# Half of the output projection in seven block products instead of eight (Strassen-Winograd) for six of sixteen tile pairs

## The reference

```python
for l in range(DEPTH):
    h = rms_norm(x, norm_g[l])
    proj = jnp.einsum('bsd,dn->bsn', h, w_in[l])
    ...
    y = jnp.concatenate([y_a, y_b, y_c], axis=-1)
    x = x + jnp.einsum('bsm,md->bsd', y, w_out[l])
return x
```

## Time and profile before

| what | value |
|---|---|
| median of three executions | 1538.51 us |
| the profiled execution, its own time | 1538.53 us |
| its span | 1536.8 us |
| PE busy | 1532.3 us (100%) |
| DVE busy | 994.8 us (65%) |
| ACT busy | 753.3 us (49%) |
| POOL busy | 356.7 us (23%) |
| HBM read and written | 219 GB/s over the span |

### The profile page before, as it was taken

How to read it: one execution, slowest core, us unless ns; L and a number is a source line. 1 busy time by engine, 2 the same in 40 slices (tenths; PEclk the granted TensorE clock), 3 DMA queues, 4 the chain that set the end, 5 groups by cost and what they waited for, 6 DMA issues and landing times.

```text
span 1536.8 us, 18847 instructions
## 1 busy us (share of the span) xinstructions
PE 1532.3 (100%) x6996; PEld 1271.5 (83%) x6996; DVE 994.8 (65%) x1537; ACT 753.3 (49%) x1006; POOL 356.7 (23%) x609
## 2 busy tenths in 40 slices
PE   9999999999999999999999999999999999999999
PEld 7888888888888888888878888888888888888887
DVE  6647555666769865576579667676456767664554
ACT  6745444587544444554554535534346444443332
POOL 9041212230230040126410354346200120200000
PEclk9999999999999999999999999999999999999999
DMA  9886778886787675558856787799875765666674
GB/s 291 283 240 193 223 211 232 212 234 192 231 244 209 195 221 162 161 185 273 246 182 188 225 244 217 227 276 260 251 245 178 255 213 192 210 198 194 194 247 156
DMA packets 206268, 337.77 MB, mean 220 GB/s; under 512 B 53050, under 2 KB 60521, under 8 KB 205921
## 3 DMA queue, kind: packets, MB, share of 16 engines
q1 hardware_dynamic: 184784, 288.66, 62.2%
q0 software_dynamic: 21344, 47.90, 10.9%
q10 hardware_dynamic: 48, 0.02, 0.0%
HBM read 312.81 MB, written 23.49 MB: 219 GB/s over the span
## 4 chain that ended last, share of the span: by engine, by line
PE 98%; DVE 1%; ACT 0%; issue 0%; DMA 0%; DVEq 0%
PE acc L1048 31%; PE acc L1051 31%; PE acc L1050 31%; PE mix L1111 1%; PE mix L1184 1%; PE mix L1104 0%; PE mix L1173 0%; PE mix L1019 0%; PE acc L1252 0%; DVE w_lo L1659 0%; PE mix L1170 0%; PE mix L1160 0%; ACT w_hi L1322 0%; PE mix L1158 0%; DMA xs<-in_x_dram 0%
## 5 line engine op out<-in xcount | busy, mean ns | idle before, releaser
L1659 DVE TENSOR_TENSOR w_lo<-w_raw,w_hi 128x1024 fp32r<-128x1024 f32 (+2 forms) x535 | 646.1, 1219 | 419.4 <-ACT w_hi L1322 416.2
L1322 ACT ACTIVATE w_hi<-w_raw 128x1024 fp32r<-128x1024 f32 (+2 forms) x535 | 556.2, 1050 | 526.5 <-PE acc L1051 460.1
L1048 PE MATMUL acc<-w_hi,op_hi 128*128 128x512 f32 (+1 forms) x2036 | 799.8, 393 | 0.3 <-DVE w_lo L1659 0.3
L1051 PE MATMUL acc<-w_hi,op_lo 128*128 128x512 f32 (+1 forms) x2036 | 792.5, 389 | 0.0
L1050 PE MATMUL acc<-w_lo,op_hi 128*128 128x512 f32 (+1 forms) x2036 | 792.2, 389 | 0.0
L1048 PEld LDWEIGHTS acc<-w_hi,op_hi 128*128 128x128 f32 x2036 | 382.4, 188 | 80.1 <-issue 1.3
L1051 PEld LDWEIGHTS acc<-w_hi,op_lo 128*128 128x128 f32 x2036 | 382.1, 188 | 79.9
L1050 PEld LDWEIGHTS acc<-w_lo,op_hi 128*128 128x128 f32 x2036 | 382.4, 188 | 77.8
L792 POOL DMA_DIRECT2D conv_dram<-y x48 | 30.6, 690 | 168.6 <-ACT y L1374 167.8
L792 POOL DMA_DIRECT2D y_dram<-y x32 | 20.5, 711 | 184.2 <-DVE y L2098 114.9
L946 POOL DMA_DIRECT2D bp_dram<-b_ps x48 | 31.4, 716 | 66.9 <-ACT b_ps L1543 62.8
(11 more groups left out here) (348 smaller groups left out, 974.3 us busy)
## 6 DMA issues: line engine op xcount, KB each, us to landing
w_raw<-in_w_in_dram SPq DMA_DIRECT2D x367, 512.0 KB, 4.5
w_raw<-in_w_out_dram SPq DMA_DIRECT2D x128, 512.0 KB, 4.4
w_raw<-in_w_in_dram SPq DMA_DIRECT2D x16, 384.0 KB, 3.3
w_raw<-in_a_wuq_dram SPq DMA_DIRECT2D x12, 512.0 KB, 5.9
conv_dram<-y POOLq DMA_DIRECT2D x48, 64.0 KB, 3.8
y<-conv_dram POOLq DMA_DIRECT2D x48, 64.0 KB, 4.5
w_raw<-in_a_wuqi_dram SPq DMA_DIRECT2D x6, 512.0 KB, 4.6
bp_dram<-b_ps POOLq DMA_DIRECT2D x48, 64.0 KB, 4.0
```

What stands on the lines that cost most here:

```text
L1048: nc.tensor.matmul(o, hi[:, kt, tok], hv[:, i, n0:n1], start=(kt == (kts if late else blk["kts"])[0]), stop=False)
L1051: last_mm = nc.tensor.matmul(o, lo[:, kt, tok], hv[:, i, n0:n1], start=False, stop=(kt == blk["kts"][-1]))
L1322: func(split_ap(w_hi, c), w_raw[:, c % RAW_BUFS, 0:n], ACT.Copy).then_inc(hi_ready, 1)
L1659: vec.tensor_tensor(split_ap(w_lo, c), w_raw[:, c % RAW_BUFS, 0:n], split_ap(w_hi, c).bitcast(F32), ALU.subtract).then_inc(lo_ready, 1)
```

## The change

The first 4 blocks of 512 output columns stay as they were (`out1`, `out2`). The other 4 become two **pairs** of blocks (4 with 5, 6 with 7), each pair worked on over all 16 pairs of k-tiles in one go, with the chunks of its two blocks in turn. So k-tiles 0 to 7 are needed at chunk 478 instead of 504. For the k-tile pairs 8 to 13 (`SEVEN`), the 2x2 products of (2 halves of tokens) x (2 k-tiles) x (2 blocks of columns) are made by 7 products and sums (Winograd's form) instead of 8: 21 matmuls for two chunks instead of 24. The rest of a pair is done plainly.

What that adds:

- `ss` and `sl`, six of each: sums of blocks of `y` (four dependent 128x128 additions on DVE, a 128x512 copy on ACT, a 128x512 subtraction on DVE), in slots 418 to 434;
- for each second chunk `c` of a seven: `seven_sums(c)` on DVE (128x1024, then 128x512, then 128x512, each waiting for the one before), made in turn `c - 4`; `t_hi`, a 128x2048 copy on ACT, in turn `c - 3`; `seven_lo(c)`, a 128x2048 subtraction on DVE, in turn `c - 2`. The chunk's own split shrinks to 128x512. There is one buffer each for `t_raw`, `t_hi` and `t_lo`;
- `evs` (eight 128x512 additions on DVE and a copy on ACT, after a pair's last seven) and `evn` (four additions at a pair's end), in place of 8 of the 16 `evac`.

The sevens' second chunks are 461, 465, 469, 473, 477, 481 and 493, 497, 501, 505, 509, 513. The semaphores of several moves are also merged into two (`brought`), to make room.

```diff
+OUT_SINGLE = 4
+PAIR_KTS = [14, 15, 8, 4, 9, 5, 10, 6, 11, 7, 12, 0, 13, 1, 2, 3]
+SEVEN = [8, 9, 10, 11, 12, 13]
...
+    weave(first + 26, [("ss", i) for i in SEVEN], 3)
+    weave(first + 27, [("sl", i) for i in SEVEN], 3)
...
                 if c >= RAW_BUFS:
-                    sp.wait_ge(lo_ready, c - RAW_BUFS + 1)
+                    d = c - RAW_BUFS
+                    if d + 1 in sevens:
+                        sp.wait_ge(t_summed, sevens.index(d + 1) + 1)
+                    else:
+                        sp.wait_ge(lo_ready, d + 1)
...
+            def seven_second(c):
...
+                three(c12, *s4, hv[:, 1], lv[:, 1], False, False)
+                pe.wait_ge(t_lo_ready, sevens.index(c) + 1)
+                three(c21, *a22, t_hi[:, 3], t_lo[:, 3], False, False)
+                three(p5, *s1, t_hi[:, 0], t_lo[:, 0], first, end_)
+                three(p6, *s2, t_hi[:, 2], t_lo[:, 2], first, end_)
+                three(p7, *s3, t_hi[:, 1], t_lo[:, 1], first, end_).then_inc(split_used, 1)
...
+                if in_seven(c) and second_col(c):
+                    func(w_hi[:, c % SPLIT_BUFS, 512:1024], w_raw[:, c % RAW_BUFS, 512:1024], ACT.Copy
+                         ).then_inc(hi_ready, 1)
+                    act.wait_ge(t_summed, sevens.index(c) + 1)
+                    if c > sevens[0]:
+                        wait_used(act, sevens[sevens.index(c) - 1])
+                    func(t_hi[:], t_raw[:], ACT.Copy).then_inc(t_hi_ready, 1)
+                    return
...
+            def seven_sums(c):
...
+                step(vec.tensor_tensor(t_raw[:, 0:2], w_raw[:, b0 + 1].rearrange("p (k n) -> p k n", k=2),
+                                       w_raw[:, b0:b0 + 2, 0:512], ALU.subtract))
+                step(vec.tensor_tensor(t_raw[:, 2], w_raw[:, b0 + 1, 512:1024], t_raw[:, 0], ALU.subtract))
+                vec.tensor_tensor(t_raw[:, 3], w_raw[:, b0, 512:1024], t_raw[:, 2], ALU.subtract
+                                  ).then_inc(t_summed, 1)
...
+            def ss(i, use):
+                a11, a21, a12, a22 = [y_columns(i)[:, P * j:P * j + P] for j in range(4)]
+                step(vec.tensor_tensor(a22, a21, a22, ALU.add))
+                step(vec.tensor_tensor(a21, a11, a21, ALU.subtract))
+                step(vec.tensor_tensor(a11, a22, a11, ALU.subtract))
+                vec.tensor_tensor(a12, a12, a11, ALU.subtract).then_inc(s_summed, 1)
...
+                if c + AHEAD - 1 in sevens:
+                    seven_lo(c + AHEAD - 1)
                 if c + AHEAD < len(chunks):
                     split_lo(c + AHEAD)
+                if c + AHEAD + 1 in sevens:
+                    seven_sums(c + AHEAD + 1)
```

More of the change, by code:

```diff
@@ L142, in plan @@
     kt_a = W_A // P
-    for n in range(D // 512):
+    for n in range(OUT_SINGLE):
         block("out1", n, "y", full[kt_a:], wide, 512, "w_out", 512 * n)
-    for n in range(D // 512):
+    for n in range(OUT_SINGLE, D // 512):
+        block("pair", n, "y", [2 * i + j for i in PAIR_KTS for j in range(2)], wide, 512, "w_out", 512 * n)
+    for n in range(OUT_SINGLE):
         block("out2", n, "y", full[:kt_a], wide, 512, "w_out", 512 * n)
@@ L149, in plan @@
     for b, blk in enumerate(blocks):
+        second = blk["kind"] == "pair" and blk["arg"] % 2
+        if second:
+            last.append(len(chunks) - 1)
+            last[b - 1] = last[b] - 1
+            continue
         for i in range(0, len(blk["kts"]), blk["per"]):
-            chunks.append((b, blk["kts"][i:i + blk["per"]]))
+            for q in range(2 if blk["kind"] == "pair" else 1):
+                chunks.append((b + q, blk["kts"][i:i + blk["per"]]))
         last.append(len(chunks) - 1)
@@ L171, in plan @@
     for b, x in enumerate(blocks):
-        woven[last[b] if b else FIRST_EVAC].append(("evac", b))
+        if x["kind"] != "pair":
+            woven[last[b] if b else FIRST_EVAC].append(("evac", b))
+        elif x["arg"] % 2:
+            of_seven = [c for c, (b_, kts) in enumerate(chunks) if b_ == b and kts[0] // 2 in SEVEN]
+            woven[of_seven[-1]].append(("evs", x["arg"] // 2 - OUT_SINGLE // 2))
+            woven[last[b]].append(("evn", x["arg"] // 2 - OUT_SINGLE // 2))
     woven[NX - 1].append(("par", 0))
@@ L229, in plan @@
     at = weave(at + 8, [[("yd", i), ("yt", i)] for i in range(4)], 2)
-    assert at <= end("out1", 7), (at, end("out1", 7))
+    first_a = next(c for c, (b, kts) in enumerate(chunks) if blocks[b]["kind"] == "pair" and kts[0] == 0)
+    assert at <= first_a, (at, first_a)
     use, order = 0, {}
@@ L408, in hybrid_kernel @@
         rows_kept = sem("rows_kept")
+        brought = [sem(f"brought{i}") for i in range(2)]
         c_rows_ready = [sem(f"c_rows_ready{i}") for i in range(2)]
@@ L1061, in _, with three, seven_first @@
             pe_done = [0]
+            def three(o, x_hi, x_lo, w_hi_, w_lo_, start, stop):
+                nc.tensor.matmul(o, x_hi, w_hi_, start=start, stop=False)
+                nc.tensor.matmul(o, x_hi, w_lo_, start=False, stop=False)
+                return nc.tensor.matmul(o, x_lo, w_hi_, start=False, stop=stop)
+            def seven_first(c):
+                p, i = pair_of(c), chunks[c][1][0] // 2
+                if p == 0:
+                    pe.wait_ge(s_lo_ready, SEVEN.index(i) + 1)
+                if i == SEVEN[0]:
+                    if p == 0:
+                        for use in four_mix(0):
+                            wait_emptied(pe, use)
+                    else:
+                        for q in range(2):
+                            pe.wait_ge(acc_read[q], (pair_block(0) + q) // 2 + 1)
+                pe.wait_ge(lo_ready, c + 1)
+                hv = split_ap(w_hi, c).rearrange("p (k n) -> p k n", k=2)
+                lv = split_ap(w_lo, c).rearrange("p (k n) -> p k n", k=2)
+                tok = slice(0, P)
+                three(seven_banks(p)[0], op_hi[:, 2 * i, tok], op_lo[:, 2 * i, tok], hv[:, 0], lv[:, 0],
+                      i == SEVEN[0], i == SEVEN[-1])
+                three(plain_banks(p)[0], op_hi[:, 2 * i + 1, tok], op_lo[:, 2 * i + 1, tok], hv[:, 1], lv[:, 1],
+                      False, False).then_inc(split_used, 1)
@@ new lines, in seven_lo, with ss @@
+            def seven_lo(c):
+                n = sevens.index(c)
+                dve.wait_ge(t_hi_ready, n + 1)
+                vec.tensor_tensor(t_lo[:], t_raw[:], t_hi[:].bitcast(F32), ALU.subtract).then_inc(t_lo_ready, 1)
+            def ss(i, use):
+                a11, a21, a12, a22 = [y_columns(i)[:, P * j:P * j + P] for j in range(4)]
[3 more added lines that the diff above has]
+                vec.tensor_tensor(a12, a12, a11, ALU.subtract).then_inc(s_summed, 1)
@@ new lines, in evn @@
+            def evn(p, use):
+                b = pair_block(p)
+                for k in range(4):
+                    if k % 2 == 0:
+                        dve.wait_ge(acc_ready, b + 1 + k // 2)
+                    dst = pair_sum(p)[:, k % 2, 512 * (k // 2):512 * (k // 2) + 512]
+                    ins = vec.tensor_tensor(dst, plain_banks(p)[k], dst, ALU.add)
+                    if p == 1:
+                        done_bank(ins, four_mix(1)[k])
+                    elif k % 2:
+                        ins.then_inc(acc_read[k // 2], 1)
+                    else:
+                        step(ins)
```

194 lines of the change are left out of this document (163 added, 31 removed).

## The result

The changed kernel takes **1552.04 us** (median of four executions, 1550.89 to 1552.47) against 1538.68 us for the kernel before in the same comparison (four, 1537.47 to 1538.88). The ratio is 1.0089, 95% interval 1.0074 to 1.0104: slower, by 13.4 us in the medians and 13.2 us in the spans (1550.0 against 1536.8). The forecast was 1551 us.

The account below looks back on a forecast made before the run. PE was taken to bound the kernel. From 1538.5 us, -8.2 for matmuls, +13.8 for the first pair and +6.6 for the sums of y made +12.2: 1551 us (own range 1547 to 1556; wider range 1541 to 1558).

Parts of the forecast that it names:

- 36 matmuls, -8.2 us: Both pairs: 36 matmuls fewer at 0.2267 us save 8.2 us, all of it counting because PE is the bound.
- Prices of the new operations: DVE and ACT: t_lo 2.30 us, t_hi 1.93, a 128-element addition 0.28, from sizes already in the trace.
- The sums of y, +6.6: Chunks 426 to 439: ss and sl overfill DVE's queue, stopping PE for 6.6 us, bounds 3.5 to 9.
- The rival in which DVE's lead takes this term: DVE's 5.5 us lead at out1's start covers most of the sums of y; 1544 us, chance 0.14.
- The first pair, +13.8: Chunks 461 to 481: other pieces inside a 10.28 us chain stop PE for 13.8 us in all.
- my range for the term: First pair's stops: 12.5 to 16 us, from bounds of t_lo, t_hi and the sums over five cycles.
- What I cost at nothing: Second pair, evs and evn, weights wanted a turn earlier, k-tiles wanted earlier, merged semaphores: all charged no time.
- Nothing for the second pair: Chunks 493 to 513: no pieces in the chain, so no stops; about 0.6 us if cycles were 0.2 longer.
- The clock: Rival: PE's clock falls in stops, twelve matmuls costing 2.4 us more; 1556 to 1558 us, chance 0.12 with other extra waits.
- my signs of being wrong: Profile: PE 100% busy, t_lo much off 2.3, DVE waiting for PE around chunk 430, matmuls 0.43 us apart after stops.

Follow-up runs that it names:

- e5: The change with sevens only in the second pair, sums of y in other slots, reload held until k-tile 13; 1533.32 us, 0.9972 of the kernel before.
- e6: The change with four sevens in the first pair, sums of y spread, seven_sums ahead of the split, reload later; 1531.34 us, 0.9958 of the kernel before.
- e2: The change with the six sums of y moved from slots 418 to 433 to others between 417 and 451; 1545.48 us, 1.0050 of the kernel before.
- e1: The change with the first pair's two reloads of x waiting until k-tile 15; 1549.45 us, 1.0075 of the kernel before.
- e3: The change with seven_sums ahead of the split in DVE's turn instead of behind it; 1547.87 us, 1.0065 of the kernel before.
- e4: The change with sevens only in the second pair, the first done plainly, sums of y left in place; 1540.38 us, 1.0017 of the kernel before.
- e7: As e6, but with six sevens in both pairs; 1538.59 us, 1.0007 of the kernel before.

## Why the prediction was right, and the step that was not

- **36 matmuls, -8.2 us**: the count is 36. e5 and e6 show the price where PE has no stop in the projection: 18 and 30 matmuls fewer gave 4.3 and 6.3 us (4.1 and 6.8 by 0.2267 us each).
- **Prices of the new operations.** `t_lo` takes 2.292 us (2.30 expected), `t_hi` 1.914 (1.93), the small additions 0.28 to 0.29 (0.28), and the split behind an `ss` waits 1.65 us (1.65). The line through three sizes in the earlier trace rows held for the fourth, four times as wide as the middle one. DVE in slot 421:

```profile
1219.80 0.28 DVE L1870 TENSOR_TENSOR y<-y 128x128 f32<-128x128 f32 x1
...
1222.71 1.23 DVE L1847 TENSOR_TENSOR w_lo<-w_raw,w_hi 128x1024 fp32r<-128x1024 f32 x1 [1.65 <-ACT w_hi L1496]
```

- **The sums of y, +6.6**: on DVE, `ap` 1 starts at 1204.21 us and `ap` 7 at 1324.53; before it was 1205.47 and 1319.13. That is 120.32 against 113.66, so 6.66 us more. The rival in which DVE's lead takes this term is out: in e2, with the sums elsewhere, the same stretch takes 113.47 us.
- **The first pair, +13.8**: from DVE's `ap` 7 to the end of the span it takes 225.47 us against 217.67, 7.80 more; with the 8.2 saved that is 16.0 us of stops, at the bound of my range for the term. By place, with 0.28 added to each row (15.5 us; half a us of the 16.0 stands beside no stop): chunk 461 1.6 us (1.4 forecast), 465 2.9 (2.9), 473 1.5 and 2.4 (2.1), 477 2.0 and 2.4 of a lower clock (4.7), 481 2.7 (2.7). So 473 is the term that was mis-sized, 3.9 us for 2.1. The first of its two stops is for the shrunken split, which I had under `t_hi` at no cost; behind `yd` 0 it comes late, but adds nothing, since `t_lo`, ready at 1373.53, holds PE until 1373.58 anyway. The failed step is in *What I cost at nothing*: "The weights: sums want a chunk one turn earlier, but it was issued three turns (8.2 us) before and lands in 4.4". The 4.4 us were a median over 128 loads, most of them with no reload beside them; from 1150 us on the loads of before took from 3.5 up to 11.6 us. The change brings the reloads of a whole pair, 1 MB in two transfers, into the first pair itself, where the chain has no slack; I charged reloads (up to 1 us) only to the stretch in which they had stood before. e1 puts the price at 1.9 us in its trace (1.7 in the medians).
- **Nothing for the second pair**: right. Its cycle is 10.27 us, PE never waits there, and `evs` and `evn` stay under cover.
- **The clock.** The rival said that a fall in the first pair shortens the next stop, and that among chunks 426 to 439 or after 481 it adds. Matmuls 0.43 us apart after a stop stood among my signs of being wrong, and they came. In the first pair the fall did what the rival said: after the stops of 1.25 and 2.15 us at 1370 and 1373 the granted clock was 0.66 over 1370 to 1380, twelve matmuls came 0.43 us apart (1.2 GHz), which is 2.4 us, and the next stop, forecast at 4.7, was 2.0: together 4.4. After 481 it adds, as the rival said: 1.5 us in e2. The traced execution of the change had no fall there. Among 426 to 439 it does not add: e3 and e4 had a fall there, the change and e1 had none, and DVE's way from `ap` 1 to `ap` 7 is 120.27 and 120.27 against 120.32 and 120.28 us. The Trainium skill (TensorE: Matmul & The Clock Gate, "HAM oscillation — how this bites in real kernels") has the array come back to half rate again and again between waits. In the ten stops of the changed kernel it did so once; the waits in that section's example are longer than any of these.

The total came out within 1.2 us because most terms of the sum were of the right size, and in part by luck: in the traced executions the late weights (+1.9) were met by an earlier start (-1.26), which has nothing to do with the change.

## What to carry to other kernels

When matmuls are traded for vector work, the question is not whether the vector engine's share has room (it was 68%, and at 87% in the second pair it held nobody up) but what stands in its queue within one lead of the bounding engine: add up that queue piece by piece, waits included, against the matmuls of the same chunks. A chain that just fits takes nothing else in, so choose how much of the trade to make stretch by stretch; four sevens where other work is woven in, and six where none is, beat both all and none. Look at every transfer that the change moves, and take the landing time from a stretch with the same traffic.

## What the runs showed of the hardware

- **The clock does not fall at every stop, nor at the same stop in every execution.** e4 and the changed kernel have the same stop in the same place, 1.84 and 1.85 us. In the change the matmuls after it come 0.23 us apart. In e4, from 1.4 us after it, seven come 0.43 us apart:

```profile
1239.77 0.50 PE L1177 MATMUL acc<-w_hi,op_hi 128*128 128x512 f32 x1 [1.84 <-DVE w_lo L1850]
...
1241.16 0.63 PE L1180 MATMUL acc<-w_hi,op_lo 128*128 128x512 f32 x1
...
1256.34 0.50 PE L1177 MATMUL acc<-w_hi,op_hi 128*128 128x512 f32 x1 [0.33 <-DVE w_lo L1850]
```

  That is 7 x 0.2 = 1.4 us. But the stop of 0.67 us at 1249.40 does not occur in e4, and that of 1.02 at 1256.14 is 0.33 there (rows above): where another engine's queue is what holds PE up, a slower PE takes it out of the next stop. Behind the last stop of a stretch, as in e2, nothing takes it back.
- **The start differs between executions by over 1 us.** In the trace of before two matmuls still take 0.85 us at 7.72 and 0.46 only at 10.42; in that of the change the same ones (L1236 is now L1407) are there at 7.43, at 0.46. PE's chain of the change:

```profile
7.43 0.46 PE acc L1407 x2
```

  At 1204 us, ahead of all that the change adds, PE is still 1.26 us ahead (its first small matmul of `ap` 1 starts at 1203.34, before at 1204.60). That is the execution and not the change: e3, the same program up to there, has two matmuls take 0.85 us as late as 7.86, and reaches this matmul 1.22 us after the change. The rows are of the change, and of e3 the second and third:

```profile
1203.34 0.38 PE L1378 MATMUL mix<-a_v,a_m 128*128 128x129 f32 x2
...
7.86 0.85 PE acc L1406 x2
...
1204.56 0.38 PE L1377 MATMUL mix<-a_v,a_m 128*128 128x129 f32 x2
```

  e6 and e7, alike up to there as well, are there at 1204.33 and 1203.07. A difference of spans of that size says nothing by itself. In e5 the same matmul starts at 1203.42, 1.18 us earlier than before, which is nearly all of the 1.2 us by which its span fell beyond its matmuls.
- **A wait of ACT can carry PE's name and be for a transfer** (1362.41, e1): the landing times of that window pointed at it, and with the two reloads moved away the same copy started 1.89 us earlier, though PE was later.
